# Runs of peer_v rows of eight instead of four in the fetch order of a hybrid decoder layer

## The reference, cut to what matters

```python
def peer_ffn(x2, peer_w_query, peer_keys1, peer_keys2, peer_u, peer_v):
    ...
    ts, j = lax.top_k(cand, PEER_TOPK)
    eidx = jnp.take_along_axis(cidx, j, axis=-1)
    g = jax.nn.softmax(ts, axis=-1)
    u = peer_u[eidx]
    v = peer_v[eidx]
    a = jax.nn.gelu(jnp.einsum('nd,nhed->nhe', x2, u).astype(jnp.float32), approximate=False)
    return jnp.einsum('nhe,nhed->nd', (g * a).astype(v.dtype), v)
```

## Time and profile before

| what | value |
|---|---|
| median of 3 executions | 2033.57 us |
| lowest, highest | 2032.26, 2042.9 us |
| the profiled execution | 2044.4 us |
| its span, first to last instruction | 2042.5 us |
| mean granted TensorE clock | 0.776 of full speed |
| TensorE matmul, VectorE, POOL busy | 63%, 63%, 57% of the span |
| moved by DMA | 691.10 MB, mean 338 GB/s |
| indirect fetches | 544 of peer_u, 544 of peer_v |

### The profile page before, as it was taken

One profiled execution on the slowest core, in us unless ns is written; L12 is line 12 of the kernel. 1 busy time (PEld: TensorE's weight loads), 2 busy tenths in 40 slices (PEclk: granted clock), 3 DMA queues, 4 the chain that ended last, 5 costly groups with the idle time before them and its releaser, 6 DMA issues.

```text
span 2042.5 us, 19255 instructions
## 1 busy us (share of the span) xinstructions
PE 1282.7 (63%) x6055; PEld 553.4 (27%) x6055; DVE 1283.9 (63%) x3066; ACT 338.4 (17%) x900; POOL 1170.4 (57%) x1127
## 2 busy tenths in 40 slices
PE   8999997976742767675466686754223234866335
PEld 4564443442401224341021352410101001221101
DVE  5338969971466767938658488385399986103341
ACT  1510021130001542110044220100000001100000
POOL 1005547745665566656656666467576677446774
PEclk9999998988965875687678757866566557899779
DMA  8819989978999899989999999799899969999997
GB/s 332 337 60 364 356 315 363 334 262 320 325 366 352 319 368 361 383 315 365 364 364 364 353 337 375 273 368 359 285 370 362 395 238 394 400 345 363 364 378 291
DMA packets 211200, 691.10 MB, mean 338 GB/s; under 512 B 27317, under 2 KB 55477, under 8 KB 204275
## 3 DMA queue, kind: packets, MB, share of 16 engines
q0 software_dynamic: 160256, 590.06, 77.3%
q1 hardware_dynamic: 43691, 90.66, 12.4%
q10 hardware_dynamic: 7152, 9.17, 1.2%
HBM read 677.27 MB, written 12.94 MB: 338 GB/s over the span
## 4 chain that ended last, share of the span: by engine, by line
DVE 31%; PE 27%; issue 13%; DMA 9%; POOL 8%; another core or an unknown queue 6%; SPq 4%; ACT 3%; DVEq 0%; ACTq 0%; POOLq 0%
DVE rings L2477 15%; POOL rings L1019 8%; PE acc L2021 6%; DMA rings<-peer_v,late 4%; PE acc L1532 4%; PE bank L1711 3%; PE acc L1499 3%; DVE small L2087 2%; DVE uah L2090 2%; SPq L810 2%; PE bank L1737 2%; SPq L802 2%; DVE zt L2287 2%; PE wide L1532 2%
## 5 line engine op out<-in xcount | busy, mean ns | idle before, releaser
L1019 POOL DMA_INDIRECT rings<-peer_u,late x544 | 615.2, 1131 | 392.8 <-DVE late L2477 145.0
L1019 POOL DMA_INDIRECT rings<-peer_v,late x544 | 533.2, 980 | 358.9 <-issue 138.8
L2021 PE MATMUL acc<-rings,z_stages 128*32 128x512 f32 x2048 | 386.7, 787 | 385.0 <-DMA rings<-peer_v,late 223.2
L2477 DVE CUSTOM_DVE_ANT_0 rings<-rings,wide 128x1024 f32<-128x1024 f32 x256 | 299.7, 1217 | 42.6 <-DMA rings<-peer_u,late 34.0
L2021 PEld LDWEIGHTS acc<-rings,z_stages 128*32 128x32 f32 x2048 | 85.7, 131 | 654.9 <-issue 652.6
L2477 DVE CUSTOM_DVE_ANT_0 rings<-rings,uah 128x1024 f32<-128x1024 f32 x160 | 191.9, 1223 | 103.5 <-DMA rings<-peer_u,late 98.8
L2477 DVE CUSTOM_DVE_ANT_0 rings<-rings,late 128x1024 f32<-128x1024 f32 x128 | 153.5, 1221 | 6.3 <-DMA rings<-peer_u,late 4.7
L1532 PE MATMUL acc<-rings 128*128 128x512 f32 (+1 forms) x352 | 152.8, 584 | 1.9 <-DMA rings<-w_in 1.9
L1867 PE MATMUL bank<-keep,soft_score 128*128 128x64 f32 x288 | 62.8, 386 | 60.9 <-issue 31.4
L1433 ACT COPY z_stages<-late 128x4 f32<-128x4 f32 x136 | 25.3, 196 | 430.2 <-PE acc L2021 187.6
L1532 PEld LDWEIGHTS acc<-rings 128*128 128x128 f32 x352 | 65.7, 200 | 73.1 <-issue 70.8
(11 more groups left out here) (316 smaller groups left out, 1686.0 us busy)
## 6 DMA issues: line engine op xcount, KB each, us to landing
rings<-w_in SPq DMA_DIRECT2D x35, 1024.0 KB, 9.0
rings<-peer_u,late POOLq DMA_INDIRECT x544
rings<-peer_v,late POOLq DMA_INDIRECT x544
rings<-w_out POOLq DMA_DIRECT2D x16, 512.0 KB
z_rows<-z_stages ACTq DMA_DIRECT2D x30, 256.0 KB
soft_score<-ln SPq DMA_DIRECT2D x6, 1024.0 KB
zt<-z_rows SPq DMA_DIRECT2D x2, 2596.0 KB
rings<-w_out POOLq DMA_DIRECT2D x4, 1024.0 KB, 7.7
```

Of the source, the lines that this page charges most:

```text
L1019: nc.gpsimd.indirect_dma_start(ring[:, place, :], None, table, offs).then_inc(row_in[place], 16)
L2021: last = nc.tensor.matmul(acc_v[QUAD * j:QUAD * (j + 1), half * BLK:(half + 1) * BLK], lone[:, quad % LONE, j, QUAD - 1 - m:2 * QUAD - 1 - m],
L2477: V.tensor_tensor_reduce(out=ring[:, place, :], in0=ring[:, place, :], in1=h, scale=1.0, scalar=0.0, op0=ALU.mult, op1=ALU.add, accum_out= ...
```

## The change

Only `fetches` changes. In each block of a mixed stage with v rows, the number of runs is now n_v // 8 instead of n_v // 4, at least one, and the v rows are shared out over the runs in whole quads. The u rows of the block are shared out over the runs as before, so there are about twice as many between two runs.

```diff
@@ -427,10 +427,11 @@
         for t in range(1, N_TILES):
             order, k, i = [], 0, EARLY_V[t - 1]
             for n_u, n_v in BLOCKS[t]:
-                runs = max(n_v // N_QUADS, 1)
+                runs = max(n_v // (2 * N_QUADS), 1)
                 for r in range(runs):
-                    order += [("v", t - 1, i + j) for j in range(N_QUADS if n_v else 0)]
-                    i += N_QUADS if n_v else 0
+                    rows = n_v * (r + 1) // runs // N_QUADS * N_QUADS - n_v * r // runs // N_QUADS * N_QUADS
+                    order += [("v", t - 1, i + j) for j in range(rows)]
+                    i += rows
                     here = n_u * (r + 1) // runs - n_u * r // runs
                     order += [("u", t, k + j) for j in range(here)]
                     k += here
```

## The result

| | before | after |
|---|---|---|
| median of 6 executions | 2041.29 us | 2052.94 us |
| lowest, highest | 2032.26, 2047.15 | 2046.7, 2072.99 |
| the profiled execution | 2044.4 | 2054.7 |
| its span | 2042.5 | 2052.7 |

The ratio is 1.0085, 95% interval 1.0049 to 1.0121. A second set of executions of the changed kernel gave 1.011 (1.0066 to 1.0154). So the change costs 0.9 to 1.1 per cent, some 17 to 23 us, where I had forecast no change.

A forecast was written before the change was run, and what follows sets the result against it. The prediction took the stream of row fetches as the bound. Its six parts, 0 - 0.04 + 0 + 0.5 - 0.2 + 0, gave +0.3 us, rounded to 0 and carried to the median: 2034 us, range 2020 to 2050.

The forecast's parts named there:

- slower rival: Stage 3, about 1510 to 1620 us: longer back-to-back dots lock POOL out, +18 us, 2052 us; chance 0.2.
- Part 1: All three stages: the same 768 fetches, the same bytes and POOL's 1.24 us each, so 0.
- Part 2: First dots of stages 1 and 2: waits change by +0.6 and +0.5, one dot saves 1.14; sum -0.04 us.
- Part 3: Tile 2 comes in at 640 us: consumers keep their order and POOL's stall ends where it did, 0.
- Part 4: Tile 3 comes in at 1012 us: earlier quad v88 to v91 costs +0.5 us, POOL's split stall wins 0.
- Part 5: Sample rows come in: two fetches ahead of the stall -2.5, nine dots instead of seven +2.3; sum -0.2 us.
- Part 6: Tile 3's dots in stage 3: longer runs hold POOL only where it would wait anyway, 0.

The follow-up runs named there:

- s1_block2: Runs of eight only in stage 1's first mixed block (10 u, 16 v), all else as the kernel before; ratio 0.9996 to the kernel before.
- s3_block4: Runs of eight only in stage 3's block of 42 u and 36 v, all else as the kernel before; ratio 0.9978 to the kernel before.
- early_before: The kernel before with the sample's small loads issued ahead of the last 16 of 64 page loads; ratio 0.9872 to the kernel before.

## Why the prediction was wrong

The forecast was no change, 2034 us; the kernel is 0.9 per cent slower, and 2052.94 lies 3 us above the range. Some 8 us of the miss are the base: in these executions the kernel before took 2041.29, not the 2033.57 that I had carried the sum over to. My slower rival gave 2052 and was given 0.2, but for a mechanism that did not decide; that it came so near is luck. One reading of mine was slightly off as well: the DMA share falls to 0.91 in a window that I did not show (865 to 973 us), not to 0.92.

**Part 1 (issue and transfer)** holds: counts, issues and bytes are the same.

**Part 2 (first rows of stages 1 and 2)** holds. The first dots of the changed kernel, in VectorE's timeline:

```profile
595.17 1.22 DVE L2478 CUSTOM_DVE_ANT_0 rings<-rings,wide 128x1024 f32<-128x1024 f32 x1 [9.70 <-DMA rings<-peer_u,late]
...
982.76 1.22 DVE L2478 CUSTOM_DVE_ANT_0 rings<-rings,wide 128x1024 f32<-128x1024 f32 x1 [4.84 <-DMA rings<-peer_u,late]
```

I had named 9.8 to 10.6 and 4.9 us; the first is just below that. s1_block2, which has stage 1's move alone, gives 0.9996.

**Part 3 (transition at 640)** is one of the two failed steps. I wrote that the stall ends where it did, and stopped there: 0. The stall did end there (POOL waits 7.85 us where the earlier trace rows have 7.95). What I had not followed were the quads behind it, v108 above all. My own rule, that each consumer moves with its fetch, was taken too far: a fetch's place is wanted 13 to 15 positions later at once, but its quad can only move where the front's pieces let it. It is the term "rest of the stage", which the sum did not have, and which measures 2.4 to 3.4 us in the traces and 7, give or take 7, in the times.

**Part 4 (transition at 1012)** holds in kind. POOL's timeline of the changed kernel has the wait for v88 at fetch 505, and a second one:

```profile
1037.16 0.94 POOL L1020 DMA_INDIRECT rings<-peer_u,late  x1 [3.31 <-PE acc L2022]
...
1064.09 1.21 POOL L1020 DMA_INDIRECT rings<-peer_u,late  x1 [5.54 <-DVE late L2478]
```

Forecast were 4 and 3 us, and that both orders meet at fetches 519 to 523. At 520 the changed kernel was 9.5 us ahead of the one before, at 540 it was 3.3 ahead. The wait before 1064.09 is that meeting. Stage 2 was not run by itself, but the traces bound it: from fetch 300 to 680 the six with the new order in stage 2 took 592.6 us on the mean, the twelve with the old one 591.4, with a standard error of 2.8 for the difference.

**Part 5 (transition at the sample rows)** is the other failed step. "Its start is SyncE's queue, whose page loads hang on no fetch" stopped too early: no wait of theirs hangs on a fetch, but I took their length as fixed, at 112.62 us, and put its change at nothing. Measured: 112.62 to 125.52 us even with the old order, 6.7 us more with the new one on the mean of the traces, 6 to 9 us in the times. The rest of this part was right in kind: the stall begins two fetches later, and eleven dots, not nine, stood back to back and held POOL's issue for 12.00 us. Against VectorE's new start, fetch 762 came 17.0 us later instead of 14.8, so +2.2 us with the two fetches counted in. By fetch 900 nothing of it is left: 248 to 254 us behind that start in six traces of the old order, 252 in all five of the new one.

**Part 6 (tile 3's dots)** holds: VectorE is busy for 146.98 of 150 us from 1500 to 1650, and s3_block4 costs nothing. The 16.58 us of the earlier trace rows stood under fifteen dots, not 14. The Trainium skill (SBUF — State Buffer, "Who interferes with whom") infers for tensor_tensor that it leaves descriptor generation alone. The dot is another instruction with two inputs in SBUF, and for it this is not borne out here: the issue under eleven dots took 12.00 us in six traces of the new order; in the two without the reads of the page table, where four dots stand back to back, the longest issue there took 5.24 and 5.56.

By the times the two steps sum to 7 us for stage 1's last block and 6 to 9 us for stage 3's second block, 13 to 16 of the 17 to 23 us measured; the difference is within the intervals. By the traces they are about 3 and 6.7 us, some 10.

Open are three things. Why ScalarE's convolution step waits for 10.39 us, with TensorE's last recorded matmul before it long over. Whether and why the page loads keep a slower pace with the new order. And where the rest of the loss is, stage 2 included.

## What to carry to other kernels

When an order of transfers changes in a ring, do not stop at the stalls that the trace shows: go through the list of places, and ask for each fetch that wants a place earlier whether the consumer of that place is free to move too, or stands behind another strand's work. A queue that waits for nothing in the moved work can still be on the path by its length, so ask how far that varies, and move what others wait for ahead of its long sequences: that alone gave 26 us here. And where traces of one kernel differ by as much as the effect, count one term over many traces at a fixed position, since each experiment brings one more trace of every part that it leaves alone. Then look where the count ends: a pause that the order shifts over its edge added 2.5 us to one here.

## What the runs showed of the hardware

**SyncE's page loads run at very different paces.** The first 48 of them with their reads of the page table took 115 us in the changed kernel, 2.4 us each, while POOL issued fetches. Once POOL stood still, SyncE's timeline has the last 16 at 0.94 us each:

```profile
1439.45 15.08 SPq L811 DMA_DIRECT2D w_query_s<-kidx_T  x16
```

POOL's issues are at most a part of this: in early_before the last 16 took 19.75 us, 1.23 each, while POOL went on issuing. Without the reads all 64 took 43.10 us beside POOL's issues, 0.67 us each. With 56 reads between the first load and the last the row is 70 to 87 us longer (112.62 and 130.16 less 43.10). The Trainium skill (DMA: Bandwidth & Descriptors, "Latency and other measured facts") gives a floor of about 600 ns for such a read; by it, as an estimate, 56 reads would add 34 us. In the changed kernel's trace the last eight reads start 0.55 us apart, near that floor, but the other sequences of eight stand 0.8 to 2.1 us apart on the mean, and what stretches them is not shown.

**A held issue is not always lost.** POOL's issue took 12.00 us under eleven dots with both operands in SBUF. It cost 2.2 us on the spot (fetch 762) and nothing that the traces show 140 fetches later. In between VectorE was the bound, busy for 146.98 of 150 us.
